# PEER expert rows read as 2 KB pieces, with four PSUM banks summed over two chunks

## What is computed

```python
act = jax.nn.gelu(jnp.einsum('nd,nhkd->nhk', xc, expert_u[idx]), approximate=False)
return jnp.einsum('nhk,nhkd->nd', g * act, expert_v[idx])
```

## Time and profile before

| | |
|---|---|
| median of three runs | 2254.78 us |
| the profiled execution, its span | 2261.95 us, 2260.3 us |
| TensorE busy over the span | 2048.5 us, 91% |
| VectorE busy over the span | 1369.1 us, 61% |
| bytes moved by DMA | 420.05 MB, mean 186 GB/s |
| down stage | from 1564.6 us (first `w_lo` of V) to the end |

### The profile page before, as it was taken

How to read it: one execution, slowest core, us unless ns; L and a number is a source line. 1 busy time by engine, 2 the same in 40 slices (tenths; PEclk the granted TensorE clock), 3 DMA queues, 4 the chain that set the end, 5 groups by cost and what they waited for, 6 DMA issues and landing times.

```text
span 2260.3 us, 39129 instructions
## 1 busy us (share of the span) xinstructions
PE 2048.5 (91%) x14822; PEld 1932.2 (85%) x14822; DVE 1369.1 (61%) x2452; ACT 729.2 (32%) x940; POOL 762.0 (34%) x493
## 2 busy tenths in 40 slices
PE   7877898678999999988999999999989889888989
PEld 6877666158999999988999999999988889878989
DVE  3768573203334587998888852000677688677775
ACT  4233565113222223322555542222222222222231
POOL 3232112322333333443122133333344344344440
PEclk9998999879999999999999999999999999999999
DMA  4333556951223334333344455335788878978874
GB/s 152 64 78 129 187 192 221 386 195 56 79 81 125 133 116 143 126 132 115 132 188 173 164 220 210 127 129 196 260 274 284 292 259 285 308 249 281 286 254 154
DMA packets 202168, 420.05 MB, mean 186 GB/s; under 512 B 28129, under 2 KB 137762, under 8 KB 189250
## 3 DMA queue, kind: packets, MB, share of 16 engines
q1 hardware_dynamic: 162866, 314.92, 40.5%
q0 software_dynamic: 32768, 100.75, 12.7%
q10 hardware_dynamic: 6416, 2.78, 0.9%
HBM read 350.46 MB, written 67.92 MB: 185 GB/s over the span
## 4 chain that ended last, share of the span: by engine, by line
issue 34%; PE 26%; DVE 12%; DMA 10%; SPq 7%; POOL 6%; ACT 3%; DVEq 2%; POOLq 1%; ACTq 0%
PE pair L1386 7%; PE pair L1387 6%; PE pair L1388 6%; DMA w_raw<-in_v_t 6%; POOL w_lo L544 5%; SPq L402 5%; DVE conv L964 3%; DVE w_lo L1330 3%; PE pair L1531 2%; DVE pair L1347 2%; ACT w_hi L856 1%; DMA page_ring<-in_cache_k 1%; DVE a_lo L1325 1%; DMA v_ring<-in_cache_v 1%; PE pair L1543 1%
## 5 line engine op out<-in xcount | busy, mean ns | idle before, releaser
L1386 PE MATMUL pair<-x_hi,w_hi 128*128 128x272 f32 x2560 | 757.8, 296 | 23.3 <-DVE x_lo L920 16.2
L1388 PE MATMUL pair<-x_hi,w_lo 128*128 128x272 f32 x2560 | 745.2, 291 | 0.0
L1387 PE MATMUL pair<-x_lo,w_hi 128*128 128x272 f32 x2560 | 743.8, 291 | 0.0
L544 POOL TENSOR_TENSOR w_lo<-w_raw,w_hi 128x2048 fp32r<-128x2048 f32 x64 | 301.6, 4713 | 623.1 <-ACT w_hi L790 623.1
L1386 PEld LDWEIGHTS pair<-x_hi,w_hi 128*128 128x128 f32 x2560 | 488.4, 191 | 26.9 <-issue 22.6
L1387 PEld LDWEIGHTS pair<-x_lo,w_hi 128*128 128x128 f32 x2560 | 488.1, 191 | 0.2
L1388 PEld LDWEIGHTS pair<-x_hi,w_lo 128*128 128x128 f32 x2560 | 487.2, 190 | 0.0
L1386 PE MATMUL pair<-a_hi,w_hi 128*128 128x416 f32 x1024 | 372.0, 363 | 71.8 <-DVE w_lo L1330 58.1
L1388 PE MATMUL pair<-a_hi,w_lo 128*128 128x416 f32 x1024 | 369.3, 361 | 0.0
L1387 PE MATMUL pair<-a_lo,w_hi 128*128 128x416 f32 x1024 | 367.0, 358 | 0.0
L1330 DVE TENSOR_TENSOR w_lo<-w_raw,w_hi 128x2048 fp32r<-128x2048 f32 x64 | 146.6, 2290 | 258.4 <-ACT w_hi L856 247.4
(11 more groups left out here) (197 smaller groups left out, 2562.3 us busy)
## 6 DMA issues: line engine op xcount, KB each, us to landing
w_raw<-in_u_t SPq DMA_DIRECT2D x64, 1024.0 KB, 5.7
w_raw<-in_v_t SPq DMA_DIRECT2D x256, 256.0 KB
acts<-act_out SPq DMA_DIRECT2D x64, 544.0 KB, 3.0
gates<-g_out SPq DMA_DIRECT2D x13, 2048.0 KB, 8.0
g_in<-gates SPq DMA_DIRECT2D x16, 1664.0 KB
act<-acts SPq DMA_DIRECT2D x64, 416.0 KB
page_ring<-in_cache_k SPq DMA_DIRECT2D x64, 256.0 KB, 3.0
page_ring<-in_cache_k POOLq DMA_DIRECT2D x64, 256.0 KB, 4.0
```

Of the source, the lines that this page charges most:

```text
L544: pool.tensor_tensor(w_lo[:, slot, :], w_raw[:, slot, :], w_hi[:, slot, :].bitcast(F32), ALU.subtract).then_inc(u_lo_done, 1)
L1386: te.matmul(out, s_hi, m_hi, start=start, stop=False)
L1387: te.matmul(out, s_hi, m_lo, start=False, stop=False)
L1388: return te.matmul(out, s_lo, m_hi, start=False, stop=stop)
```

## The change

V is read in rows of 2 KB. A chunk now holds 512 outputs (four blocks, `q` 0 to 3) of only two of the quad's steps. It is still 1 MB, there are still 64, and it is loaded with two DMAs of 512 KB. Chunks 0 and 1 of a quad (first and last two steps) give blocks 0 to 3, chunks 2 and 3 give blocks 4 to 7. The even chunk (`piece` 0) starts the sums in banks 0 to 3, the odd one (`piece` 1) completes them in the same banks. Each chunk still has 48 matmuls, each quad eight additions. All four additions of a pair come after the odd chunk's quarters: `add_block(c, 0)` and `(c, 1)` ahead of `low_acts`, `(c, 2)` behind it, `(c, 3)` at the head of the next iteration; even iterations have none of their own. `turn_rows` stands ahead of the last quarter.

```diff
-            v_parts = io["v_t"].rearrange("(u s) p (j h d) -> u h p s j d", s=4, j=2, h=4)
+            v_parts = io["v_t"].rearrange("(u g s) p (j h d) -> u h g p s j d", g=2, s=2, j=2, h=2)
             def load_v(quad, part):
-                for x in range(4):
-                    sp.dma_start(w_raw[:, part % 2, WC // 4 * x:WC // 4 * (x + 1)].rearrange("p (j d) -> p j d", j=2),
-                                 v_parts[quad, part, :, x]).then_inc(v_loaded[part % 2], 16)
+                for x in range(2):
+                    sp.dma_start(w_raw[:, part % 2, WC // 2 * x:WC // 2 * (x + 1)].rearrange("p (j d) -> p j d", j=2),
+                                 v_parts[quad, part // 2, part % 2, :, x]).then_inc(v_loaded[part % 2], 16)
...
-                    sc.wait_ge(down_done, 2 * c + 2)
-                    high_v(c + 2, k % 2, 256 * it + 64 * (k // 2) + 128)
+                    sc.wait_ge(down_done, 4 * c + 4)
+                    high_v(c + 2, k % 2, 128 * it + 32 * (k // 2) + 64)
...
-            def add_block(c, o):
-                db = 2 * (c % 4) + o
-                v.wait_ge(down_done, 2 * c + o + 1)
-                v.tensor_tensor(resid[:, db, P:N], resid[:, db, P:N], bank(db % 4)[:, 0:ND], ALU.add)\
-                    .then_inc(added, 1)
+            def add_block(c, q):
+                db = 4 * (c % 4 // 2) + q
+                v.wait_ge(down_done, 4 * c + q + 1)
+                v.tensor_tensor(resid[:, db, P:N], resid[:, db, P:N], bank(q)[:, 0:ND], ALU.add).then_inc(added, 1)
...
-                if c:
-                    add_block(c - 1, 1)
+                if c and c % 2 == 0:
+                    add_block(c - 1, 3)
...
-                add_block(c, 0)
+                if c % 2:
+                    add_block(c, 0)
+                    add_block(c, 1)
                 if c + 4 < STEPS:
                     low_acts(c + 4)
+                if c % 2:
+                    add_block(c, 2)
...
-            add_block(STEPS - 1, 1)
+            add_block(STEPS - 1, 3)
...
-                for o in range(2):
-                    if last_chunk and o == 1:
+                piece = part % 2
+                for q in range(4):
+                    if last_chunk and q == 3:
                         turn_rows()
-                    wait(te, added, 2 * c + o - 3)
-                    for t in range(8):
-                        col = 2 * P * t + P * o
-                        stationary = (w_hi[:, part % 2, col:col + P], w_lo[:, part % 2, col:col + P])
-                        last = product(bank((2 * part + o) % 4)[:, 0:ND], stationary,
-                                       (a_hi[parity][:, t, :], a_lo[parity][:, t, :]), t == 0, t == 7)
+                    if piece == 0:
+                        wait(te, added, 2 * c + q - 3)
+                    for t in range(4):
+                        col = CH * t + P * q
+                        stationary = (w_hi[:, piece, col:col + P], w_lo[:, piece, col:col + P])
+                        last = product(bank(q)[:, 0:ND], stationary,
+                                       (a_hi[parity][:, 4 * piece + t, :], a_lo[parity][:, 4 * piece + t, :]),
+                                       piece == 0 and t == 0, piece == 1 and t == 3)
                     last.then_inc(down_done, 1)
```

More of the change, by code:

```diff
@@ L875, in _ @@
             sc.wait_ge(up_done, 2 * STEPS - 2)
-            high_v(0, 0, 64)
+            high_v(0, 0, 32)
             for j in range(2):
@@ L879, in _ @@
             sc.wait_ge(up_done, 2 * STEPS)
-            high_v(1, 1, 64)
+            high_v(1, 1, 32)
             def down_step(it, k, last=False):
```

## The result

The changed kernel takes 2265.19 us, median of six runs (2261.54 to 2271.78), the kernel before 2255.22 in the same runs: ratio 1.0049, 95% interval 1.003 to 1.0068. Run beside the first experiments it was 2264.36 against 2254.97 (1.0059, 1.0037 to 1.0081). So the change costs about 10 us, with both intervals together 7 to 18; 8.7 was forecast. One execution of a later experiment (four issues) took 3664 us at a lower granted clock and is left out of its median.

A forecast was written before the change was run, and what follows sets the result against it. The down stage was taken as bound by a chain through SP, DMA and DVE over late V loads. Turns +5.6, after V(54) +0.8 and the end +2.3 gave +8.7 us, 2263.5 on the median 2254.78; range 2243 to 2275.

The forecast's parts named there:

- The loop: Down stage: a chain through SP, DMA and DVE over two late even V loads sets the quad's 43.64 us, 13 turns.
- The new wait of PE: Late even chunk: PE waits for the odd chunk's first addition, restarting 1.9 us later; a floor of +0.26 us on one leg.
- The 1.5 us: Late chunk's PE time: the two chunks after a long wait take about 1.5 us over 2 x 9.1.
- Two additions ahead of `low_acts`: DVE, odd iterations: one more addition delays the activations' load, and V behind it on SP, by 0.50 us per leg.
- V(4k+2) leg: Turn's part up to the V load behind the gates: +0.50 for the addition, -0.33 for packets, +0.17 us.
- V(4k) leg: Turn's other part, up to the next quad's first V load: +0.17 us, raised to +0.26 by PE's wait.
- 2 KB packets: V loads: half as many packets per chunk save 0.33 us; bounds 0.50 gained to 0.18 lost.
- under 16.2: V load behind the gates: landing in under 16.2 us would make the forecast wrong; about 16.9 was expected.
- After V(54): Last chunks, PE the limit: V(56) comes one addition later, about +0.8 us (0 to 1.2).
- The end: Last chunk: `turn_rows` moves from half to three quarters, so sum and stores come later, +2.3 us.
- Issue time: Rival, V loads on SP: two issues for four land V behind the gates 1.80 us sooner; 2244 us, chance 0.26.
- PE's wait as the whole 1.9 us in each turn: Rival, PE's restart: lower clock for longer, or the delay reaching the next load, costs 25 us; 2283 us, chance 0.09.

The follow-up runs named there:

- the first experiments: Three changed-kernel variants: first addition ahead of the split (2254.94 us), second addition behind `low_acts` (2258.32), fetched rows turned at half of the last chunk (2262.20).
- the wait alone: Kernel before, with PE also waiting ahead of every even chunk for the first addition of the odd chunk just before it: 2263.79 us against 2254.89.
- the three traces: Two traces of the changed kernel, and one of it with fetched rows turned at half of the last chunk (2262.20 us).
- the loads alone: Changed kernel with the first addition ahead of the split and fetched rows turned at half of the last chunk: 2250.81 us against 2254.89.

## Why the prediction was right, point by point

**The loop.** Right. The turn goes through two even loads, and its longest part is the 17 us behind the gates; cutting the gates freed 68 us, inside the range that was written down for it.

**The new wait of PE.** Its place and the 1.9 us were right (1.93), its price on the leg was not: a floor of +0.26 us was worked out, +1.04 measured. The step that failed is the end of the late chunk, 9.1 + 1.5 = 10.6 us. From the restart to `w_hi` of V(4k) it is 10.7 to 12.2 us in the changed kernel, mean 11.5; with the 1.93 that gives 13.4 to 13.5 of the leg's 13.57. The 1.5 us stood for the lower clock: 3.0 us at half clock in the turn that was read, 3.2 in the mean before the change. They were carried over unchanged to a PE that stands longer and restarts later, and there it is 4.3 us in the mean, 2.8 to 6.1 in single turns, which is 0.6 of the 0.9 us that are missing. Most of the rest is the 0.35 us of the last matmul's own length and the release, which were left out. It is not simply the length of the stop: behind one of 5.78 us there were 3.8 us at half clock (1848.31), behind one of 3.80 us there were 6.1 (1890.37). Also, the one turn that was read had V(24) landing late (12.66 us for the leg, mean 12.53). The run with the wait alone puts 8.9 us on it, where the floor gives 0.26 x 13 = 3.4.

**Two additions ahead of `low_acts`.** 0.50 us was right (the "x2" row). Moving the second one back gave 6.0 us, for the V(4k+2) legs of 13 turns 0.46 each: right. On the V(4k) leg it is covered by PE's wait, in 11 of 12 legs of that run: also as written.

**2 KB packets.** The term was mis-sized on one side and right on the other. On SP's DMA queue, 1632 to 2155 us, before and after (packets, MB, share):

```profile
q1 hardware_dynamic: 85500, 91.30, 53.3%
```

```profile
q1 hardware_dynamic: 59328, 91.24, 49.8%
```

The same bytes took 3.5% of 523 x 16 us less, 293 us of one engine, over 12 quads of four chunks: 0.38 us a chunk on 16 engines, where 0.33 was worked out. Not all of it need be the packets: the changed kernel also has two issues for four. With four issues of the same 2 KB rows the queue took 51.2% for 90.55 MB, 47.3 us of one engine for a MB, where it is 48.9 before and 45.7 after; by this one trace about half of the 0.38 is the packets. Going to two issues of 1 KB rows, however, saved nothing (53.3% for 91.08 MB, 49.0). (The estimate of 0.14 us from the packet cost in the Trainium skill, "DMA: Bandwidth & Descriptors", "Why small descriptors are slow", is under the 0.38, and near the half of it.) But V alone, before and after, 2221 to 2227 us:

```profile
q1 hardware_dynamic: 544, 1.05, 55.0%
```

51.4 us of one engine before, 0.55 x 6 x 16 = 52.8 now: on this one chunk nothing is saved when nothing else runs. The leg gains look larger than the packets: V(4k+2) was 16.95 us from issue to `w_hi` and is 16.26, 15.96 and 16.52 in the three traces, 0.4 to 1.0 less. The prediction had named under 16.2 as what would make it wrong, and one of the three is there; but the experiment with the wait alone has 16.60 with 1 KB rows, so some of this is the coupling and not the packets. Also, V is issued only 0.12 to 0.20 us later on this leg, not 0.50, as SP gets from the gates to V sooner (0.82 us from issue to issue in the mean of 13 turns, 1.17 before). So the V(4k+2) leg, forecast at +0.17, came out at -0.31 to -0.79. In all the loads were worth 4.1 us by the run of the loads alone, of 8.6.

**After V(54).** +0.8 was forecast and can't be told. From `w_lo` of chunk 54 to that of chunk 63 it is 84.17 us before and 84.92, 83.25 and 85.13 in the three traces.

**The end.** +2.3 forecast; +2.22 measured from PE's last matmul to the end of the span (6.47 against 4.25), and 2.2 between the medians.

**Sum.** Wait and additions together 9.4, the end 2.2, the loads -2 to -4, gives 8 to 10; forecast 8.7 from terms that were each smaller on both sides (wait and additions net of the loads 5.6, the next leg 0.8, end 2.3). The prices do not simply add: the wait alone costs 8.9 and the second addition 6.0, but taking both away gives 9.4. That the total came so near is partly luck. Per turn +0.26 and +0.17 were forecast for the two legs and +1.04 to +1.14 and -0.31 to -0.79 measured; the sum, +0.43, is inside the +0.12 to +0.67 of the turn. Two errors cancel: the wait was taken too low, and the gain of the V(4k+2) leg too.

**The rivals.** Issue time: out, by the two runs with other numbers of issues. The rule of the Trainium skill that went with it ("DMA: Bandwidth & Descriptors", "Bandwidth": larger DMAs come nearer to the peak) did not hold for the kernel before, where DMAs of 512 KB in place of 256 made it slower (2261.4 us); for 2 KB rows no run tells them apart. PE's wait as the whole 1.9 us in each turn: out, 8.9 us and not 25. But it was nearer to the truth in kind than the forecast, which had PE's wait as a small floor: its condition, that PE runs at the lower clock for longer after the longer stop, is met in the mean (4.3 us in place of 3.2), though only by about 1 us of PE's time in a turn (6.0 to 6.5 us at half clock in place of 4.3), and not by 3.7.

## What to carry to other kernels

When sums are closed over two chunks in the same banks, look at what now stands between "input ready" and "bank free" on the engine that does both; here one fetched row and one addition behind a late split cost nearly as much as the whole change. If the change makes an engine stand longer, don't carry over the length of the work behind the stop from the old trace: here the late chunk had 4.3 us at half clock and not 3.2, and 10.7 to 12.2 us from turn to turn. Put the addition that frees the first bank ahead of the step that announces the late input. Above all, find the lump: a transfer of 1.6 MB in front of a 1 MB one that everybody waits for was worth 68 us, more than ten times what the size of the rows moved.

## What had not been expected

- A load with full DMA engines has an elastic leg: with one leg 0.9 us longer, fetched rows of 0.25 MB more passed on it, and the next leg had 0.12 MB less to move and was 0.5 us shorter (wait alone, one trace of each).
- With packets of 2 KB and two issues for four, a chunk saves 0.38 us of the 16 engines in traffic, and one chunk alone saved nothing (52.8 against 51.4 us of one engine).
- With PE's restart 1.8 us later, the late chunk spent 4.3 us at half clock in place of 3.2 (a whole turn 6.0 to 6.5 in place of 4.3).
- One 512 KB DMA for every second KB of the slot is slower than two of 256 KB with the same packets: 2261.4 against 2254.2 us. Its cause is open.
